# Forgetting attention: dividing the gate instead of the probabilities

## What is computed

```python
def block(args):
    qb, cb, start = args
    q_pos = start + jnp.arange(FOX_BLOCK, dtype=jnp.int32)
    logits = (jnp.einsum('bhqd,bhkd->bhqk', qb, k).astype(jnp.float32) * scale
              + cb[..., :, None] - c[..., None, :])
    mask = key_pos[None, :] <= q_pos[:, None]
    probs = jax.nn.softmax(jnp.where(mask, logits, -jnp.inf), axis=-1)
    return jnp.einsum('bhqk,bhkd->bhqd', probs.astype(v.dtype), v)
...
o = fox_attention(qh, kh, vh, log_f.transpose(0, 2, 1))
o = o.transpose(0, 2, 1, 3).reshape(b_, s_, FOX_WIDTH)
return (o * jax.nn.silu(g)) @ w_out
```

## Time and profile before

| | |
|---|---|
| time before, median of 3 runs | 2405.28 us (2401.43 to 2405.4) |
| the profiled execution's own time | 2401.78 us |
| span of its instructions | 2399.8 us |
| busy: PE, PEld, DVE, ACT, POOL | 93%, 78%, 47%, 34%, 23% of the span |
| mean granted TensorE clock | 0.97 of full speed |

### The profile page before, as it was taken

How to read it: one execution, slowest core, us unless ns; L and a number is a source line. 1 busy time by engine, 2 the same in 40 slices (tenths; PEclk the granted TensorE clock), 3 DMA queues, 4 the chain that set the end, 5 groups by cost and what they waited for, 6 DMA issues and landing times.

```text
span 2399.8 us, 29628 instructions
## 1 busy us (share of the span) xinstructions
PE 2228.7 (93%) x11452; PEld 1867.6 (78%) x11452; DVE 1133.2 (47%) x1614; ACT 810.4 (34%) x1241; POOL 558.4 (23%) x292
## 2 busy tenths in 40 slices
PE   4899998999999699999899979999999999978996
PEld 4678887788887598899778868778778778766885
DVE  6953232442431733343435453564655555554444
ACT  3134544112012323323323134454454454443311
POOL 1321221333433022222233222111111111112320
PEclk9999999999999699999999989999999999998998
DMA  8111112111431111111131121001001001003101
GB/s 335 44 46 69 70 70 71 44 36 53 163 143 44 80 40 40 36 36 36 36 149 38 42 97 55 36 26 44 35 26 44 35 26 44 35 18 132 44 18 70
DMA packets 33459, 150.38 MB, mean 63 GB/s; under 512 B 3777, under 2 KB 3777, under 8 KB 31330
## 3 DMA queue, kind: packets, MB, share of 16 engines
q1 hardware_dynamic: 23840, 93.52, 10.8%
q10 hardware_dynamic: 9538, 55.68, 6.1%
HBM read 128.15 MB, written 21.04 MB: 62 GB/s over the span
## 4 chain that ended last, share of the span: by engine, by line
PE 82%; DVE 11%; issue 4%; ACT 2%; DMA 0%; POOL 0%; DVEq 0%; SPq 0%; ACTq 0%; POOLq 0%
PE psG L310 21%; PE psG L312 21%; PE psG L311 21%; PE psA L310 3%; PE psA L1745 3%; PE psA L312 2%; PE psA L311 2%; DVE FTL L2024 1%; PE psA L1729 1%; PE psA L1728 1%; PE psA L1652 1%; DVE FP L2009 1%; DVE M L860 1%; DVE AL L813 1%; PE psA L398 1%
## 5 line engine op out<-in xcount | busy, mean ns | idle before, releaser
L310 PE MATMUL psG<-AH,WH 128*128 128x512 f32 x2112 | 855.4, 405 | 64.1 <-DVE AL L813 29.0
L312 PE MATMUL psG<-AH,WL 128*128 128x512 f32 x2112 | 834.2, 395 | 0.0
L311 PE MATMUL psG<-AL,WH 128*128 128x512 f32 x2112 | 833.4, 395 | 0.0
L297 POOL TENSOR_SCALAR WH<-RAW 128x1024 fp32r<-128x1024 f32 x144 | 168.3, 1169 | 1754.9 <-PE psG L310 1284.8
L310 PEld LDWEIGHTS psG<-AH,WH 128*128 128x128 f32 x2112 | 403.2, 191 | 154.0 <-issue 29.8
L312 PEld LDWEIGHTS psG<-AH,WL 128*128 128x128 f32 x2112 | 402.3, 190 | 88.2
L311 PEld LDWEIGHTS psG<-AL,WH 128*128 128x128 f32 x2112 | 404.2, 191 | 73.7
L299 POOL TENSOR_TENSOR WL<-RAW,WH 128x1024 fp32r<-128x1024 f32 x144 | 390.3, 2710 | 12.0
L1895 ACT ACTIVATE FTH<-psA 128x512 fp32r<-128x512 f32 (+1 forms) x160 | 88.6, 554 | 199.3 <-PE psA L1745 198.6
L2024 DVE TENSOR_TENSOR FTL<-psA,FTH 128x512 fp32r<-128x512 f32 (+1 forms) x160 | 102.0, 637 | 102.2 <-ACT FTH L1895 99.4
L2009 DVE CUSTOM_DVE_ANT_0 FP<-psA,CB 128x256 f32<-128x256 f32 (+7 forms) x128 | 96.9, 757 | 70.1 <-PE psA L1731 69.7
(11 more groups left out here) (305 smaller groups left out, 2980.8 us busy)
## 6 DMA issues: line engine op xcount, KB each, us to landing
RAW<-w_tiles SPq DMA_DIRECT2D x144, 512.0 KB, 3.2
gates<-SIG ACTq DMA_DIRECT2D x16, 512.0 KB, 2.9
park<-X ACTq DMA_DIRECT2D x2, 4096.0 KB, 11.1
CB<-fox_c ACTq DMA_DIRECT2D x8, 1024.0 KB, 4.6
X<-xT SPq DMA_DIRECT2D x4, 1024.0 KB, 12.0
WADA_SCALE<-w_ada SPq DMA_DIRECT2D x1, 4096.0 KB, 24.2
WADA_SHIFT<-w_ada SPq DMA_DIRECT2D x1, 4096.0 KB, 33.9
WADA_GATE<-w_ada ACTq DMA_DIRECT2D x1, 4096.0 KB, 16.4
```

The costliest lines, as they stand in the source:

```text
L297: nc.gpsimd.tensor_scalar(WH[:, i, :], RAW[:, i % RAW_SLOTS, :], 1.0, 0.0, ALU.mult, ALU.add).then_inc(w_high, 1)
L310: first = nc.tensor.matmul(out, wh, xh, start=start, stop=False)
L311: nc.tensor.matmul(out, wh, xl, start=False, stop=False)
L312: return first, nc.tensor.matmul(out, wl, xh, start=False, stop=stop)
```

## The change

The probabilities stay undivided. `divide` keeps only the reciprocal, and `turn(i, 0)` waits for the exponentials alone. Behind the last `weigh` of each block TensorE transposes the two columns of reciprocals, each spread over 128 columns, into columns 256 to 511 of the same bank, so that each partition has the reciprocals along the row. `out(i)` first multiplies the gate with them, waits for its own result, and then multiplies with the output of the attention as before.

```diff
         def turn(i, x):
             g = AT_PART[i] + x
             if x == 0:
-                pe.wait_ge(fp_ready, p * N_S + (2 * i + 2))
+                pe.wait_ge(fexp_done, p * N_S + (2 * i + 2))
...
                 _, l = three(psA[:, 3, 0:2 * P], FVH[:, n, :], FVL[:, n, :], FTH[:, g % 2, ts], FTL[:, g % 2, ts], n == 0, n == i)
+            if x + 1 == PARTS[i]:
+                pe.wait_ge(frd_ready, p * N_S + (2 * i + 2))
+                for r in range(2):
+                    s = 2 * i + r
+                    l = nc.tensor.transpose(psA[:, 3, (2 + r) * P:(3 + r) * P], FRD[:, s % 4:s % 4 + 1].to_broadcast([P, P]), mat("ident"))
             l.then_inc(fpv_done, 1)
...
             dve.wait_ge(fexp_done, p * N_S + (s + 1))
             nc.vector.reciprocal(FRD[:, s % 4:s % 4 + 1], FDEN[:, s % 4:s % 4 + 1]).then_inc(frd_ready, 1)
-            dve.wait_ge(frd_ready, p * N_S + (s + 1))
-            probs = FP[:, i % 2, r, 0:(i + 1) * P]
-            nc.vector.tensor_scalar(probs, probs, FRD[:, s % 4:s % 4 + 1], None, ALU.mult).then_inc(fp_ready, 1)
...
             dve.wait_ge(fpv_done, p * N_PARTS + (AT_PART[i] + PARTS[i]))
             if i == 0:
                 dve.wait_ge(psum_free, u + 4)
+            for r in range(2):
+                hs = slice(64 * r, 64 * r + 64)
+                y = Y[hs, bass.ds(p, 1), i * P:(i + 1) * P].rearrange("p a f -> p (a f)")
+                l = nc.vector.tensor_tensor(y, psA[hs, 3, (2 + r) * P:(3 + r) * P], y, ALU.mult)
+            l.then_inc(fgate_scaled, 1)
+            dve.wait_ge(fgate_scaled, p * NB + (i + 1))
             for r in range(2):
                 hs = slice(64 * r, 64 * r + 64)
                 y = Y[hs, bass.ds(p, 1), i * P:(i + 1) * P].rearrange("p a f -> p (a f)")
```

More of the change, by code:

```diff
@@ L1624, in build @@
     frd_ready = sem("frd_ready")
-    fp_ready = sem("fp_ready")
+    fgate_scaled = sem("fgate_scaled")
     ft_full = sem("ft_full")
```

## The result

| | before | after |
|---|---|---|
| time, median | 2403.93 us of 4 runs | 2440.7 us of 4 runs (2435.36 to 2442.07) |
| ratio | | 1.015, 95% interval 1.0131 to 1.0169 |
| profiled execution: span, mean granted clock | 2399.8 us, 0.970 | 2437.7 us, 0.969 |
| PE, DVE busy | 2228.7 us, 1133.2 us | 2244.8 us, 1099.9 us |

The account below looks back on a forecast made before the run. TensorE, the busiest engine, was taken to be paced by two nearly equal paths through VectorE. Seven pairs at 4.47 us (31.3) plus 6.1 in the last made 37.4 us, so 2440 us; likeliest 2431 to 2450, whole range 2424 to 2452.

Parts of the forecast that it names:

- two paths nearly equally long: Between VectorE and TensorE in each block: the change shortens one path and lengthens the other, so pairs get 4.47 us longer.
- the second path: score(i+2, 0) - peak - `out` - `low` - `turn(i+1, 1)`: lengthened, as `out` grows by 0.62 us.
- the first path: score - peak - division - `turn(i, 0)`: shortened, since TensorE's wait for the division goes (9.9 us in all).
- the 1.25 us that the forecast had given back: All that is given back in a loop pair, subtracted from the added transposes and longer `out`.
- The three signs of being wrong: Peak earlier than 0.19 us behind its scores, `out` under a microsecond, or the wait only moving to `turn(i, 1)` unchanged.
- the four waits of 1.0 to 1.5 us that were forecast: TensorE's waits for `FTL` at each of `turn(3, 1)` to `turn(6, 1)` in a pair.
- The transposes were put at 0.25 us: Price on TensorE of each block's two added transposes with the return, from 0.20 to 0.31 us.
- 0.87 a block twice: Blocks 4 to 5 and 5 to 6: transposes and longer `out` add fully, nothing given back; delay 3.10, then 3.97 us.
- a tenth each for two parts of `low`: Two parts of `low` behind a division may win a tenth each; left out of the sum.
- A: Rival: the clock falls too, one half-clock stretch in most pairs adds 10 us, 2450 us; chance 0.08.
- B: Rival: added products hide in VectorE's idle time and nothing changes, 2402 to 2410 us; chance 0.11 including a half-way case.
- C: Rival: faster, transposes at most 0.11 us and `out` hidden, each pair wins 0.9 us, 2398 us; chance 0.05.

Follow-up runs that it names:

- i: Changed kernel with `out` of blocks 2 to 5 moved ahead of `peak(i+2, 0)` on VectorE, all added work kept; 2403.1 us.
- c: Changed kernel without the transposes of the reciprocals and without the gate's products with them, so no division at all; 2396.7 us.
- b: Changed kernel without the transposes of the reciprocals; `out` still multiplies the gate twice, with the attention's output; 2432.4 us.
- a: Changed kernel without the gate's products with the reciprocals; the transposes are made but not read; 2408.2 us.
- l: i, with `out(1)` also moved, from ahead of `peak(2, 1)` to behind it and the reciprocal (2, 0); 2400.1 us.
- j: Kernel before, division kept, with `out` of blocks 3 to 5 moved ahead of `peak(i+2, 0)`, behind the division (i+1, 1); 2398.9 us.
- m: j, with L813 moved ahead of `peak(i+2, 0)` in the last pair; 2389.6 us.
- p: l, with L813 moved ahead of `peak(i+2, 0)` in the last pair; 2394.3 us.
- k: Changed kernel with the sixteen sum matmuls of block 7 issued in two halves with a slice behind each; 2440.9 us.

## Why the prediction was right

**The path.** The step that carried the forecast held: two paths nearly equally long, of which the change shortens the first and lengthens the second. i shows it for the second path. With `out` moved off it, the waits of TensorE at the transposes fell from 36.2 to 7.9 us, although every added instruction was still made. c shows the first path alone. Of the 1.25 us that the forecast had given back, 1.08 came from the missing division up to `turn(4, 1)` (0.65, 0.22, 0.10 and 0.11); c is 1.08 earlier there. The three signs of being wrong stayed away: the peak starts 0.18 us behind its scores where 0.19 was named, which is the last digit of the rows, `out` takes 1.24 us, and the wait at `turn(4, 1)` is 1.22 us instead of the 0.43 that stood at `turn(4, 0)`. Of the four waits of 1.0 to 1.5 us that were forecast, the one at `turn(6, 1)` is 0.81.

**The prices.** `out` grew from 0.61 to 1.24 us, as worked out, and enters six times a pair (b). The idle time ahead of the second product, which waits for the first, is 3.1 us for 128, 0.024 each and less than the 0.035 behind the reciprocal. The transposes were put at 0.25 us and are 0.21 by the pairs of a and c. At one place the two take 0.14 us from start to start, and the first matmul behind them 1587.51 - 1587.25 = 0.26, where its equal after it takes 0.17. From PE's timeline of the changed kernel, in block 1 of the second pair:

```profile
1587.11 0.38 PE L1760 MATMUL psA<-MATS,FRD 128*128 128x128 f32 x2
1587.25 0.42 PE L1728 MATMUL psA<-FKA,FX 128*128 128x384 f32 x1
1587.51 0.34 PE L1729 MATMUL psA<-FKB,FX 128*128 128x384 f32 x1
1587.68 0.22 PE L1731 MATMUL psA<-FHIDE,IDR 128*128 128x128 f32 x1
```

The Trainium skill's estimate for a product (VectorE: DVE Perf Modes, The TRN2 errata), 0.26 us, is below the 0.288 of the rows after, as it was below those of before.

**The delays step by step.** The second pair begins 1572.63 - 1569.66 = 2.97 us later than before, by the start of its V transposes; this is taken off below. PE's timeline of the changed kernel has that start, `weigh(1, 0)` and `turn(2, 0)`:

```profile
1572.63 1.04 PE L1781 MATMUL psA<-MATS,VF 128*128 128x128 f32 x8
...
1586.31 0.38 PE L310 MATMUL psA<-FTH,FVH 128*128 128x256 f32 x1 [0.39 <-DVE FTL L2026]
...
1590.25 0.66 PE L1745 MATMUL psA<-MATS,FP 128*128 128x128 f32 x4 [0.39 <-ACT FP L1891]
```

And these are `turn(5, 1)` and `turn(6, 1)` of the same pair, before and then after the change:

```profile
1610.10 0.66 PE L1745 MATMUL psA<-MATS,FP 128*128 128x128 f32 x4 [0.68 <-DVE FTL L2024]
...
1619.75 0.66 PE L1745 MATMUL psA<-MATS,FP 128*128 128x128 f32 x4 [0.18 <-DVE FTL L2024]
```

```profile
1615.94 0.65 PE L1745 MATMUL psA<-MATS,FP 128*128 128x128 f32 x4 [1.37 <-DVE FTL L2026]
...
1626.32 0.66 PE L1745 MATMUL psA<-MATS,FP 128*128 128x128 f32 x4 [0.81 <-DVE FTL L2026]
```

`weigh(1, 0)` is 1586.31 - 1582.58 - 2.97 = 0.76 late (forecast 0.70), `turn(2, 0)` 1.03 (0.92), and `turn(4, 1)` 1606.79 - 1601.62 - 2.97 = 2.20 (2.23). From there the forecast added 0.87 a block twice, with nothing given back, and came to 3.10 and 3.97; `turn(5, 1)` is 2.87 late and `turn(6, 1)` 3.60. A pair without a stretch at half the clock ended 4.0 us longer and not 4.47. Two terms were mis-sized. The transposes are 8 x 0.04 us cheaper. And the missing division gave back some 0.3 more in blocks 4 to 6: c, 1.08 us earlier at `turn(4, 1)`, is 1.4 earlier at the end of the pair. The forecast had left out a tenth each for two parts of `low` that stand behind a division; the rest of the 0.3 has no row of its own. The first two blocks were some 0.1 later than forecast, against it; no run shows a cause for that.

**The total.** It was forecast at 37.4 us, and the profiled spans differ by 37.9. Part of that closeness is luck: the seven pairs gave 7 x 4.0 = 28 us for themselves instead of 31.3; two more stretches at half the clock added 3.2; what comes from the start of the last pair's V transposes on is 7.6 us longer (301.6 against 294.0) where 6.1 were forecast, and a part of it is the clock as well, with a mean of 0.93 against 0.94; and the program ahead of the pairs was 1.0 us shorter in this execution.

**The rivals.** A was half right: the clock did fall more often, at the price per stretch that the earlier trace rows suggest, but in three pairs and not in most. That the longer waits brought it on is not shown: l, j and m, whose longest wait in the seven pairs is 0.7 us, have two such stretches each. B and C are out for this order of instructions. i (2403) and l (2400) land near their times of 2402 to 2410 and 2398, but that is no proof of their sums: the transposes cost 0.21 us and not the 0.11 that C needed, the added products still cost 0.9 us a pair in l, and the early place won some 0.9 us a pair with the old products alone (j).

## What to carry to other kernels

An instruction that is cheaper in sum can be dearer in its place. Before moving work from one instruction of an in-order engine to another, write down what stands behind each on that engine, and who waits for that: here 74 us ahead of one wait were exchanged for 37 us ahead of a more pressing one.

When a wait is removed, follow the next instruction of the waiting engine to its next wait. Here it came two slices later, and took back 0.5 of the 1.6 us won up to there (c).

Where an addition turns out to be on the path, try its other places before giving it up. Two orders of the same instructions lie 37 us apart here (changed kernel and i, some 5 of them by the clock), the two ways of dividing at their best places 1 to 5 (l against j, p against m).

## What the hardware showed beyond that

Runs of the kernel before spread by 0.3% and those of i by 0.5%, and the spread goes with TensorE's mean granted clock: the kernel before had a span of 2398.5 us at 0.971 and of 2405.3 at 0.967, i one of 2392.9 at 0.974 and one of 2405.5 at 0.968. The program ahead of the pairs is the same in all thirteen kernels, and in the profiled executions it took from 1479.3 us (i, at 0.97) to 1485.9 us (l, at 0.96). Stretches at 1.2 GHz, some 3 us long, fall in the first pair of one kernel and the fifth of another, each while TensorE is fed and right behind the sixteen matmuls of two columns. In k, with these in two halves, the loop had none, and as much was lost behind it. A gain or loss of 2 or 3 us in the profile of one execution can be no more than that.
